# The samples of a decode step: weights as the stationary operand, or 32 rows of activations in four column tiles

## What is computed

```
h  = h + concat(o_a, o_b) @ w_out                        # 2048 x 2048, output projection
hf = rmsnorm(h, g_ffn)
h  = h + (silu(hf @ w_gate) * (hf @ w_up)) @ w_down      # 2048 -> 5632 -> 2048
y  = rmsnorm(h, g_final)
```

## Time and profile before

| | |
|---|---|
| median of 3 runs | 1766.61 us (1765.39 to 1831.78) |
| profiled execution | 1762.6 us, span of its slowest core 1760.9 us |
| spans of the eight cores | 1748.1 to 1760.9 us |
| mean granted TensorE clock | 0.983 to 0.987 |
| TensorE busy | 1670.9 us (95%) |
| DVE, ACT, POOL busy | 29%, 29%, 9% |
| samples' output projection L1251, core 7 | 256 matmuls, busy 6.9 us |
| samples' down matmuls L1341 | 704 matmuls, busy 19.0 us |
| norms of the samples L1204 | 64 records, busy 7.3 us |

### The profile page before, as it was taken

The page is one execution under the profiler, slowest core; times in us unless marked ns, Lnnn a source line. Parts: engine busy times, 40 slices in busy tenths (PEclk is TensorE's granted clock), DMA queues, the critical chain, the costliest instruction groups (busy, mean ns, idle before and its releaser), DMA issues.

```text
span 1760.9 us, 33110 instructions; the slowest of 8 cores (1748.1 to 1760.9 us)
## 1 busy us (share of the span) xinstructions
PE 1670.9 (95%) x13836; PEld 1186.3 (67%) x13836; DVE 513.5 (29%) x940; ACT 518.5 (29%) x977; POOL 153.5 (9%) x112
## 2 busy tenths in 40 slices
PE   2699999998998979999999999999999999999998
PEld 2587676676664544456666666666666689999997
DVE  3408826567563443432111111111111100000015
ACT  3527537676664765111010010010100101101012
POOL 1000210112222000001010100101010000000000
PEclk9899999999999999989999999999999999999999
DMA  9866556676879934329756659585766466666665
GB/s 217 195 102 133 92 73 96 124 120 124 158 152 194 236 78 112 138 99 137 97 64 81 73 72 132 59 94 60 85 70 75 48 111 94 91 90 91 91 115 195
DMA packets 268048, 196.72 MB, mean 112 GB/s; under 512 B 5211, under 2 KB 256603, under 8 KB 263567
## 3 DMA queue, kind: packets, MB, share of 16 engines
q0 software_dynamic: 210304, 111.15, 52.1%
q1 hardware_dynamic: 57309, 82.41, 15.2%
q10 hardware_dynamic: 288, 1.05, 0.1%
HBM read 271.11 MB, written 27.91 MB: 170 GB/s over the span
## 4 chain that ended last, share of the span: by engine, by line
PE 88%; DMA 4%; DVE 2%; ACT 2%; issue 1%; SPq 1%; POOL 0%; ACTq 0%; DVEq 0%; POOLq 0%
PE PS L634 50%; PE PS L1319 17%; PE PS L1179 6%; PE PS L522 3%; PE PS L554 3%; DMA arena<-w_in 2%; PE PS L717 2%; PE PS L1004 1%; SPq L978 1%; PE PS L1341 1%; PE PS L463 1%; DMA arena<-xall 1%; DMA arena<-arena 1%; PE PS L878 0%; PE PS L1204 0%
## 5 line engine op out<-in xcount | busy, mean ns | idle before, releaser
L634 PE MATMUL PS<-arena 128*128 128x344 bf16 (+4 forms) x6144 | 923.6, 311 | 10.8 <-DVE arena L961 10.0
L634 PEld LDWEIGHTS PS<-arena 128*128 128x128 bf16 x6144 | 596.9, 98 | 317.2 <-issue 13.7
L1319 PE MATMUL PS<-arena 128*128 128x256 bf16 x2816 | 309.0, 273 | 0.0
L1319 PEld LDWEIGHTS PS<-arena 128*128 128x128 bf16 x2816 | 274.9, 98 | 31.8
L1275 DVE TENSOR_TENSOR arena<-PS,arena 128x352 bf16<-128x352 f32 (+1 forms) x132 | 68.6, 520 | 544.5 <-PE PS L634 539.2
L1273 ACT ACTIVATE arena<-PS 128x352 f32<-128x352 f32 (+1 forms) x132 | 60.7, 460 | 554.4 <-PE PS L634 554.4
L1179 PE MATMUL PS<-arena 128*128 128x512 bf16 x512 | 115.0, 384 | 2.0 <-ACT arena L1029 1.7
L1328 ACT ACTIVATE arena<-arena 128x256 bf16<-128x256 f32 x64 | 26.7, 417 | 287.6 <-DVE arena L1326 287.6
L1326 DVE TENSOR_TENSOR arena<-PS,arena 128x256 f32<-128x256 f32 x64 | 27.2, 425 | 257.0 <-PE PS L1319 249.4
L1179 PEld LDWEIGHTS PS<-arena 128*128 128x128 bf16 x512 | 50.3, 99 | 62.5 <-issue 5.8
L345 POOL DMA_DIRECT2D arena<-w_gate x22 | 25.1, 1143 | 707.4 <-PE PS L634 492.8
(11 more groups left out here) (155 smaller groups left out, 1124.8 us busy)
## 6 DMA issues: line engine op xcount, KB each, us to landing
arena<-w_in POOLq DMA_DIRECT2D x32, 1024.0 KB, 12.3
arena<-xall SPq DMA_DIRECT2D x24, 1024.0 KB, 9.8
arena<-w_gate POOLq DMA_DIRECT2D x22, 1024.0 KB, 14.0
arena<-w_up POOLq DMA_DIRECT2D x22, 1024.0 KB, 16.9
arena<-w_down POOLq DMA_DIRECT2D x8, 2816.0 KB, 25.7
arena<-arena SPq DMA_DIRECT2D x128, 65.8 KB, 5.3
arena<-sh SPq DMA_DIRECT2D x16, 512.0 KB, 4.5
shn<-arena SPq DMA_DIRECT2D x16, 512.0 KB, 5.4
```

The source lines that it names most:

```text
L634: ins = e.matmul(ps(b)[:, 0:n], wv[:, k, m * 128:(m + 1) * 128], src3[:, k, c0:c0 + n], start=(k == 0), stop=(k == 15))
L1319: ins = e.matmul(ps(b)[:, 0:256], hm3[:, k, ti * 128:ti * 128 + 128], wv[:, k, :], start=(k == 0), stop=(k == NFF - 1))
```

## The change

The samples go over to the orientation of the rows. Columns 1008 to 1039 of `mix3` or `hm3` (16 last prompt rows and the 16 samples, 32 in all; the results of the first 16 are not used) are the stationary operand, and the weights are streamed.

- In the output projection there is one matmul for each k and each column block `cb` of 512, four of them next to each other in four column tiles: block `cb` ends up on partitions 32cb to 32cb + 31. The result `h4` is 128 x 512. The norm's sum of squares is taken along the free dimension by ACT, and one f32 matmul with `gsel` (ones where the row indices agree modulo 32) adds the four partial sums. The normalised values are transposed back by four transposes and four DVE multiplications into `hf3`.
- In the down stage, block k goes to column tile k mod 4, so that the four tiles hold four partial sums of the same 256 columns. DVE copies them out of PSUM, an f32 matmul with `gsel` adds them, and DVE adds the right 32 partitions to `h4`.
- `xs4`, `gf4` and `ys4` (128 x 512) replace `xsT` and `ysT` (128 x 256) as input, gain and output; the memset of `onesf` gives way to a load of `gsel`.

```diff
+    for k in range(16):
+        for cb in range(4):
+            ins = e.matmul(ps(b)[32 * cb:32 * cb + 32, :], mix3[:, k, 1008:1040],
+                           w3(wo[cb], 512)[:, k, :], start=(k == 0), stop=(k == 15))
-    for c in range(16):
-        for k in range(16):
-            ins = e.matmul(ps(b)[:, c * 16:c * 16 + 16],
-                           w3(wo[c // 4], 512)[:, k, (c % 4) * 128:(c % 4) * 128 + 128],
-                           mix3[:, k, 1024:1040], start=(k == 0), stop=(k == 15))
...
+        def samples_rstd(src, junk, b):
+            op("act", lambda e: e.activation(out=junk.b, in_=src.f, func=AF.Square, accum_out=rs16.f[:, 0:1]), [src.r],
+               [junk.r, rs16.s(0)], cost=.8)
+            op("pe", lambda e: e.matmul(ps(b)[:, 0:1], gsel.f, rs16.f[:, 0:1], start=True, stop=True),
+               [gsel.r, rs16.s(0)], px=[b], cost=.3)
+            rstd(rs16.f[:, 1:2], [rs16.s(1)], ps(b)[:, 0:1], [], [b], 1, 1.0 / D)
...
+                op("dve", lambda e: e.tensor_scalar(out=xn4.b, in0=h4.f, scalar1=rs16.f[:, 1:2], scalar2=None,
+                                                    op0=ALU.mult), [h4.r, rs16.s(1)], [xn4.r], cost=.4)
+                    for j in range(4):
+                        ins = e.transpose(out=psb(b)[:, j * 128:(j + 1) * 128], in_=xn4.b[:, j * 128:(j + 1) * 128],
+                                          identity=identb.b)
...
-                for c in range(2):
-                    for k in range(NFF):
-                        ins = e.matmul(ps(7)[:, c * 16:c * 16 + 16], wv[:, k, c * 128:(c + 1) * 128],
-                                       hm3[:, k, 1024:1040], start=(k == 0), stop=(k == NFF - 1))
+                for k in range(NFF):
+                    q = k % 4
+                    ins = e.matmul(ps(7)[32 * q:32 * q + 32, 0:256], hm3[:, k, 1008:1040], wv[:, k, :],
+                                   start=(k < 4), stop=(k >= NFF - 4))
+            op("pe", fn, [w.r] + [hmid.s((fc, 2)) for fc in range(NFF)], px=[7], cost=1.3)
+            op("dve", lambda e: e.tensor_copy(out=tS.f, in_=ps(7)[:, 0:256]), [], [tS.r], px=[7], cost=.42)
+            op("pe", lambda e: e.matmul(ps(7)[:, 256:512], gsel.f, tS.f, start=True, stop=True), [gsel.r, tS.r],
+               px=[7], cost=.45)
+            p0, c0 = 32 * (cb // 2), 256 * (cb % 2)
+            op("dve", lambda e: e.tensor_tensor(out=h4.f[p0:p0 + 32, c0:c0 + 256], in0=ps(7)[p0:p0 + 32, 256:512],
+                                                in1=h4.f[p0:p0 + 32, c0:c0 + 256], op=ALU.add), [h4.r], [h4.r],
+               px=[7], cost=.42)
```

More of the change, by code:

```diff
@@ L294, in build_nc @@
     xall = dt("xall", [2110, D], F32, kind="ExternalInput").ap()
-    xsT_d = dt("xsT", [128, 256], F32, kind="ExternalInput").ap()
+    xs4_d = dt("xs4", [128, 512], F32, kind="ExternalInput").ap()
+    gsel_d = dt("gsel", [128, 128], F32, kind="ExternalInput").ap()
+    gf4_d = dt("gf4", [128, 512], F32, kind="ExternalInput").ap()
     sh = dt("sh", [16, 8, 128, 128], F32, kind="ExternalInput").ap()
@@ L1156, in build_nc @@
         hf3 = hfT.b.rearrange("p (k t) -> p k t", t=1040)
-        hsT = T(52728, 256)
-        hs2 = T(50024, 256)
-        xsT = T(50280, 256)
+        h4 = T(cst.lo + C_RM + 128, 512)
+        tS = T(52728, 256)
+        xs4 = T(50024, 512)
+        xn4 = T(50536, 256)
+        sq4 = T(50792, 256)
         OB = [0, 1, 2, 3, 4, 5]
-        onesf = calloc(128)
+        gsel = calloc(128)
         mixall = [mixT.s(c) for c in range(16)]
@@ L1170, in stream_D @@
             return wD[i], w3(wD[i], 256)
-        op("dve", lambda e: e.memset(onesf.f, 1.0 / 128), [], [onesf.r], cost=.2)
-        dma("sp", xsT.f, xsT_d, wr=[xsT.r], key="xsT", nb=131e3)
+        dma("sp", gsel.f, gsel_d, wr=[gsel.r], key="gsel", nb=65e3)
+        dma("sp", xs4.f, xs4_d, wr=[xs4.r], key="xs4", nb=262e3)
         def out_mm(ti, cb, b, ks, first, last):
@@ new lines, in so @@
+                    return ins
+                op("pe", so, mixall + [w.r for w in wo], px=[b], cost=3.6)
+                op("dve", lambda e, b=b: e.tensor_tensor(out=h4.f, in0=ps(b), in1=xs4.f, op=ALU.add),
+                   [xs4.r], [h4.r], px=[b], cost=.7)
+                b = nxt("tb", [6, 7])
+                samples_rstd(h4, sq4, b)
+                op("dve", lambda e: e.tensor_scalar(out=xn4.b, in0=h4.f, scalar1=rs16.f[:, 1:2], scalar2=None,
+                                                    op0=ALU.mult), [h4.r, rs16.s(1)], [xn4.r], cost=.4)
@@ new lines, in build_nc, with st @@
+                b = nxt("tb", [6, 7])
+                p4 = psb(b)[:, 0:512].rearrange("p (j c s) -> p j c s", c=4, s=32)
+                def st(e, b=b):
+                    ins = None
+                    for j in range(4):
+                        ins = e.transpose(out=psb(b)[:, j * 128:(j + 1) * 128], in_=xn4.b[:, j * 128:(j + 1) * 128],
+                                          identity=identb.b)
+                    return ins
+                op("pe", st, [xn4.r, identb.r], px=[b], cost=.4)
@@ L1261, in build_nc @@
+                for j in range(4):
+                    op("dve", lambda e, j=j, p4=p4: e.tensor_tensor(
+                        out=hf3[:, j::4, 1024:1040], in0=p4[:, j, :, 16:32],
+                        in1=vec.f[:, V_GFFN + j:V_GFFN + 16:4].unsqueeze(2).to_broadcast([128, 4, 16]),
+                        op=ALU.mult), [vec.r], [hfT.s(8)], px=[b], cost=.25)
         hmid = T(2200, 22880)
@@ L1393, in build_nc @@
                 dma("sp", gfin.f, gfin_d, wr=[gfin.r], key="gfin", nb=1.05e6)
[L1394 to L1397, removed]
+                gf4 = T(49656, 512)
+                sqf = T(50168, 256)
+                y4 = T(50424, 512)
+                dma("sp", gf4.f, gf4_d, wr=[gf4.r], key="gf4", nb=262e3)
+                samples_rstd(h4, sqf, 7)
+                op("dve", lambda e: e.scalar_tensor_tensor(out=y4.f, in0=h4.f, scalar=rs16.f[:, 1:2], in1=gf4.f,
+                                                           op0=ALU.mult, op1=ALU.mult), [h4.r, gf4.r, rs16.s(1)],
+                   [y4.r], cost=.7)
+                dma("sp", ys_d, y4.f, rd=[y4.r], key="ys", nb=262e3)
             for ti in range(8):
@@ L1475 @@
     gfin = np.ascontiguousarray(np.broadcast_to(np.asarray(norm_final_g, f32)[None, :], (128, D)))
+    gsel = np.ascontiguousarray(np.tile(np.eye(32, dtype=f32), (4, 4)))
+    gf4 = np.ascontiguousarray(np.repeat(np.asarray(norm_final_g, f32).reshape(4, 512), 32, axis=0))
     wrep = np.ascontiguousarray(np.tile(cw[0:30], (4, 1)))
@@ L1494 @@
         xall = np.ascontiguousarray(np.concatenate([xpre[::-1], xpre[1010:1040], xmain, xs], axis=0))
-        xsT = np.ascontiguousarray(xs.reshape(16, 16, 128).transpose(2, 1, 0).reshape(128, 256))
+        xs4 = np.zeros((4, 32, 512), f32)
+        xs4[:, 16:32] = xs.reshape(16, 4, 512).transpose(1, 0, 2)
         in_maps.append({
-            "xall": xall, "xsT": xsT,
+            "xall": xall, "xs4": xs4.reshape(128, 512), "gsel": gsel, "gf4": gf4,
             "sh": np.ascontiguousarray(state_hgrn[0, 16 * c:16 * c + 16]),
```

13 lines of the change are left out of this document (2 added, 11 removed).

## The result

The changed kernel is faster: the ratio to the kernel before is 0.988, with a 95% interval of 0.9838 to 0.9922. Its undisturbed executions took 1743.26 and 1746.36 us, those of the kernel before 1765.39 and 1766.61; in the others one die or both ran at a lower clock for a while, and they are left out of every ratio here. The two that are left average 1744.8 and 1766.0, a gain of 21.2 us. The gain is 1.2%, and less than 2% was forecast. In two further comparisons the ratio was 0.9884 (0.987 to 0.9898) and 0.9922 (0.9905 to 0.9938).

The account below looks back on a forecast made before the run. TensorE, busy 95% of the span, was taken as the bound. Core 2's gains, 9.0 + 2.1 + 3.3 = 14.4 us, put the slowest core at 1746.0, 14.9 less; the median 1766.6 became 1752, range 1745 to 1761.

Parts of the forecast that it names:

- the base of the sum: Whole kernel: profiled execution 1762.6 us would become 1747.7; the median, 1766.6, lies 4 above and is moved equally.
- The terms of the output stage: From projection to FFN: 33.5 us after the change, a gain of 10.1 on core 7 and 9.0 on core 2.
- The cover: Output projection: 16 matmuls (3.45 us) before each dependent step hide DVE and ACT work; without them some 3 us idle.
- here the clock did not fall, so no clock is to be won back: Down stage, behind the second norm: 264 matmuls take 28.84 us, 109.2 ns each, so the clock offers no gain.
- The gain of the down stage: Down stage: a slice costs 1.95 us for 2.21, eight give back 2.1; the last norm gives 3.3.
- The cores end within a few tenths of each other: End of kernel: core 7 at 1760.9 us, core 2 at 1760.4; a gain on core 7 alone counts half a microsecond.
- Unhidden loads: Down stage and projection: each weight load adds 28 ns, 11.6 us in all, giving 1763; chance 0.08, wholly or partly.
- Low clock after the change: Output projection: the 3.0 us of clock stay and the projection takes up to 3.5 more, giving 1758; chance 0.06.
- L1004 runs at 1.00 and behind it too: Convolution: matmuls of the same tiled form keep the granted clock at 1.00, an argument against the clock staying low.
- Tiles in turn: Down stage: column tiles do not run side by side at 256 columns; a slice 5.4 us for 2.21, 1780; chance 0.02.
- Slower by DVE's copy: Down stage: the f32 matmul waits for DVE's copy, 0.42 us; a late copy would hold the next seven tiles.
- loading and streaming are equal at 256 columns: Down stage: 28 ns per load against 27 per stream, so nothing is spare; it spoke for loads not being hidden.

Follow-up runs that it names:

- before_again: The kernel before, unchanged, with a second profile and five more times; ratio to the kernel before 1.0001.
- before_new_inputs: The kernel before with only a load of the norm's constant in place of the memset and the changed kernel's input sizes; ratio 0.9998.
- after_again: The changed kernel, unchanged, with a second profile and five more times; ratio to the kernel before 0.9884.
- down_one_tile: The changed kernel with the samples' 44 down matmuls all in one column tile, without copy and f32 matmul; one execution, 1775.71 us.
- down_half_columns: The changed kernel with only 128 of the 256 columns moved per sample matmul of the down stage; one execution, 1740.56 us.
- before_split_projection: The kernel before with the samples' 256 narrow projection matmuls cut into four pieces of 64 behind row tiles 2 to 5; ratio 0.9996.
- before_short_norm: The kernel before with DVE adding the 16 feature blocks and one f32 matmul in place of 16 in both norms; ratio 0.9952.

## Why the prediction was wrong

The forecast is 7.2 us above the measured 1744.8. The failed steps account for part of it: the gain in the stages was put 1.3 us too small (14.9 for 16.2; the eight slices gave 0.8 more than forecast and the clock behind the last norm 0.7), and the base of the sum 3.1 us too high. The two timed executions of the changed kernel were 2.2 us faster than its average over all comparisons. The rest is rounding and scatter.

**The terms of the output stage were right.** 33.5 us was forecast for the stretch from the projection to the FFN, and 33.44 was measured: 3.57 + 0.11 for the projection (3.67 forecast), 0.12 for the row sums (0.22, taken from L1204's run of sixteen), 0.22 for the four transposes, and the clock at 1.00. The mean over the cores went from 133.0 to 123.8, 9.2 us, where 9.0 was forecast for core 2. The cover held: no TensorE wait shows between the samples' steps, on any core.

**The first step that failed is "here the clock did not fall, so no clock is to be won back".** It was read on core 7 and taken for the kernel. Ten of the 24 cores in three profiles of this code lose 1.67 us behind the last norm, core 4 in the profile at hand among them. That is 0.7 us in the mean over the cores. On the time it acts only where the slowest core is among them: in before_again it was (core 7, 330.2 us), in the first profile and in before_new_inputs it was not. The term that was put at nothing is thus worth 0 to 1.7 us of an execution.

**The gain of the down stage was forecast a little small.** 1.31 + 0.11 + 0.43 = 1.85 a slice against 1.95 forecast, so 8 x (2.21 - 1.85) = 2.9 us in place of 2.1, and the norm 3.36 in place of 3.3. With the clock the down stage gave back 329.3 (the mean of the three profiles of before) - 322.3 = 7.0 us, where 5.4 was forecast.

**The second step that failed is the base of the sum.** "The median of the runs is 1766.6, 4 above it, and I move it by the same amount": those 4 us between the profiled execution and the median were taken as belonging to the kernel. The 49 executions of the kernel before that count in a ratio, over all comparisons, took 1758.2 to 1768.2 us, 1763.5 in the mean, and only seven of them 1766.6 or more. From 1763.5 the same sum gives 1748.6. The same reading took the cores for level: "The cores end within a few tenths of each other" holds for the two slowest of eight, whose spans are 1748.1 to 1760.9, and which core is the slowest changes from one execution to the next.

**What is left is scatter, and the range had too little room for it.** The stages give 9.2 + 7.0 = 16.2 us, a ratio of 0.991. The three comparisons gave 0.988, 0.9884 and 0.9922, around 21, 20 and 14 us. Taken together, the ten such executions of the changed kernel took 1743.3 to 1753.9 us, 1747.0 in the mean, 16.5 below the 1763.5 of before: on the average the time follows the stages. The prediction gave a gain above 20 us 4 in 100, by its costs, and the first comparison shows one of 21.2 that the stages do not have. With the other two ratios 1766.6 would become 1746.1 and 1752.8, both inside the range. So the side of 1745 on which the time fell is chance; 1752 itself would have been reached by luck too, since the base was 3.1 us high and the gain too small. On a single core the start of the output stage moves by 9 us, and the FFN takes 621.8 us on most cores but 630.1 on one core of after_again. The range of the forecast was built from the bounds of the costs alone. Why two comparisons came out some 5 and 3 us beyond the sum of the stages, and the third 2 short of it, stays open: their intervals do not all overlap, so executions of one comparison are more alike than those of different ones, and no run singles out a cause.

**The rivals.** Unhidden loads: refuted by down_one_tile and down_half_columns. The rule of "TensorE: Matmul & The Clock Gate", Part 3, in the Trainium skill, that a load overlaps with running matmuls only in another row group, does not hold for these runs: all of them share one, and 44 matmuls in one column tile take their streaming time, 109.2 ns each. Low clock after the change: refuted, 1.00. "L1004 runs at 1.00 and behind it too" was read at 639 us only; at 661 us, behind a wait of 7.94 us for a transfer, the granted clock was 0.50. Tiles in turn: absent. In down_one_tile the 44 take 4.91 us; with the 0.43 of the f32 matmul a slice would be 5.3, where 5.4 was forecast. Slower by DVE's copy: never late, TensorE does not wait for it on any core. The single number "loading and streaming are equal at 256 columns" was wrong by a factor of 1.7 or more (28 ns for a load, where a load and its matmul together take 16.6), without harm, since streaming was the greater anyway.

## What to carry over

Few rows against large weights: make the rows the stationary operand, stream the weights, and put four 32-column blocks side by side; the price was a quarter of the streaming time and 0.1 us each for the way into the form and out of it. Before turning anything round, look for runs of narrow matmuls and for slow rows behind them: two small repairs in the old orientation gave back ten of the sixteen microseconds. Read a suspected clock fall on every core, not on the slowest one, and the time before from more than three executions. A gain of 16 us in a kernel whose executions lie 10 us apart is read better from the stages of a trace than from a few times.

## What the runs showed that was not expected

- The clock fell behind 16 f32 matmuls of 16 columns (3.48 us) at the end of the kernel on 10 of 24 cores in three profiles, and on 5 of 8 in before_split_projection, and not on the others: 30.51 or 28.84 us for the next 264 matmuls. What decides it on a core stays open. Cut down to one such matmul (0.13 us) it fell on none.
- 88 narrow matmuls in a row (2.21 us) and 64 (1.60 us) between dense work never brought it down; 256 (6.5 to 8.5 us from the first start to the last) did on every core: over the stretch from 745 to 800 us, the norm included, the clock of the 24 cores was 0.91 to 0.94, and 0.94 to 0.97 on the eight of before_short_norm.
- With column tiles, 44 load and matmul pairs of 128 columns take 0.73 us, 16.6 ns a pair, where the narrow pairs with 128-column loads need 25 (2.21/88).
- One f32 matmul of one column takes 0.12 us and one of 16 columns 0.13, but 16 of 16 columns take 3.48, 0.22 each. That the f32 loads set this pace is argued, not tried.
